# A transformer block pair: the recurrent branch's next projections move into its batches, its block ends into the next preparation, and two attention heads share an output

## What is computed

```python
h = rmsnorm(x, g_mix); z = h @ w_in                      # w_in: 1024 x (672 + 1792 + 2048)
z_mla, z_rwkv, z_gate = split(z)
y_a = mla_branch(z_mla, ...)       # 8 heads: causal softmax(q k^T * scale) @ v, head width 96, v 64
y_b = rwkv7_branch(z_rwkv, ...)    # 8 heads of 64: S_t = S_{t-1} diag(d_t) + (S_{t-1} a_t) b_t^T + v_t k_t^T ; y_t = S_t r_t
gate_a, gate_b = split(sigmoid(z_gate))
x = x + (gate_a * y_a + gate_b * y_b) @ w_out
```

## Time and profile before

| | |
|---|---|
| median of 3 runs | 4001.68 us (3997.36 to 4002.08) |
| the profiled execution | 4002.18 us, span 4000.9 us |
| PE busy | 3722.5 us, 93% of the span |
| DVE, ACT, POOL busy | 45%, 33%, 29% |
| mean granted TensorE clock | 0.957 of full |
| recurrent branch, stages | 49.8 to 1002 us of the span |
| attention | 1107 to 1351 us |

### The profile page before, as it was taken

How to read it: one execution, slowest core, us unless ns; L and a number is a source line. 1 busy time by engine, 2 the same in 40 slices (tenths; PEclk the granted TensorE clock), 3 DMA queues, 4 the chain that set the end, 5 groups by cost and what they waited for, 6 DMA issues and landing times.

```text
span 4000.9 us, 44744 instructions
## 1 busy us (share of the span) xinstructions
PE 3722.5 (93%) x18398; PEld 3068.7 (77%) x18398; DVE 1807.8 (45%) x2380; ACT 1319.3 (33%) x2129; POOL 1167.1 (29%) x624
## 2 busy tenths in 40 slices
PE   5898898979899999999999898999988899999998
PEld 4786887878877777888888666777666778888886
DVE  3435444444155544323332453897543444343435
ACT  3323232232344333122122344776123233232322
POOL 3322313231100232333333112666133322232321
PEclk8988898988999999999999999999999999999999
DMA  4101010000100353111111123222354431111111
GB/s 117 57 1 54 1 47 19 19 29 18 40 12 1 97 162 98 50 48 48 50 50 48 63 90 95 79 74 92 96 159 146 138 95 48 48 48 48 48 48 53
DMA packets 282075, 253.65 MB, mean 63 GB/s; under 512 B 11333, under 2 KB 221569, under 8 KB 281872
## 3 DMA queue, kind: packets, MB, share of 16 engines
q1 hardware_dynamic: 267264, 216.52, 17.9%
q10 hardware_dynamic: 11520, 25.17, 1.6%
q0 software_dynamic: 3088, 9.10, 0.6%
HBM read 214.04 MB, written 36.70 MB: 63 GB/s over the span
## 4 chain that ended last, share of the span: by engine, by line


## 5 line engine op out<-in xcount | busy, mean ns | idle before, releaser
L401 POOL TENSOR_TENSOR weight_lo<-stage,weight_hi 128x1024 fp32r<-128x1024 f32 (+4 forms) x265 | 630.7, 2384 | 1492.9 <-ACT weight_hi L393 1465.3
L364 PE MATMUL psum<-hT_hi,weight_hi 128*128 128x512 f32 x2240 | 893.3, 399 | 13.5 <-ACT sig_g L744 6.6
L365 PE MATMUL psum<-hT_lo,weight_hi 128*128 128x512 f32 x2240 | 879.8, 393 | 0.0
L366 PE MATMUL psum<-hT_hi,weight_lo 128*128 128x512 f32 x2240 | 879.3, 393 | 0.0
L364 PEld LDWEIGHTS psum<-hT_hi,weight_hi 128*128 128x128 f32 x2240 | 426.3, 190 | 111.4 <-issue 14.1
L365 PEld LDWEIGHTS psum<-hT_lo,weight_hi 128*128 128x128 f32 x2240 | 426.1, 190 | 93.2 <-issue 5.8
L366 PEld LDWEIGHTS psum<-hT_hi,weight_lo 128*128 128x128 f32 x2240 | 425.2, 190 | 89.7
L393 ACT ACTIVATE weight_hi<-stage 128x1024 fp32r<-128x1024 f32 (+4 forms) x329 | 315.6, 974 | 466.0 <-PE psum L366 406.6
L1937 DVE TENSOR_TENSOR x<-x,psum 128x512 f32<-128x512 f32 x432 | 289.9, 686 | 215.3 <-PE psum L366 214.7
L364 PE MATMUL psum<-weight_hi,act_hi 128*128 128x512 f32 x864 | 339.2, 393 | 0.0
L366 PE MATMUL psum<-weight_hi,act_lo 128*128 128x512 f32 x864 | 338.9, 392 | 0.0
(11 more groups left out here) (371 smaller groups left out, 5955.3 us busy)
## 6 DMA issues: line engine op xcount, KB each, us to landing
stage<-in_w_in SPq DMA_DIRECT2D x64, 512.0 KB, 4.0
stage<-in_w_up SPq DMA_DIRECT2D x44, 512.0 KB, 3.9
scratch_gates<-gate ACTq DMA_DIRECT2D x64, 256.0 KB, 2.0
gs<-scratch_gates SPq DMA_DIRECT2D x64, 256.0 KB, 2.8
stage<-in_w_out SPq DMA_DIRECT2D x32, 512.0 KB, 4.6
stage<-in_w_ffn_up SPq DMA_DIRECT2D x32, 512.0 KB, 4.1
stage<-in_w_ffn_down SPq DMA_DIRECT2D x32, 512.0 KB, 3.8
stage<-in_w_down SPq DMA_DIRECT2D x22, 512.0 KB, 3.3
```

Of the source, the lines that this page charges most:

```text
L364: q.matmul(out, stat[0], mov[0], start=first, stop=False)
L365: q.matmul(out, stat[0], mov[1], start=False, stop=False)
L366: return q.matmul(out, stat[1], mov[0], start=False, stop=final)
L401: g.q.tensor_tensor(lo, K.staged(w), hi.bitcast(F32), ALU.subtract).then_inc(*S.w_lo_pool.up(w))
```

## The change

- **Recurrent branch.** The z stage of block b+1 leaves its place. Its steps are put behind steps of the batches of block b (`order_batches`): r's first half behind the second `gram` of the first two batches, r's second half and its weight step behind `first`, r's mix behind level 2's product, k's first half behind `carry`; in the other two batches k's second half and weight step behind the second `gram`, k's mix behind level 1, v's halves behind level 3's product and behind `carry`, v's mix at the end. In block 3's batches four gate halves take these places. The end of block b (`finish_0` to `finish_4`) is put between the steps of the preparation of block b+1 (`order_prep`); the waits for the yT store go into a `finish_4` of their own behind the transposes. Gate halves: 6, 8, 6, 6 in the preparations, 4 in the last batches, 2 with the last end. The handover in front of each preparation but the first is that of the batches' end; the one before block 0's z projections and the one behind them go away.
- **Ring.** The weight ring has three slots until the branch ends, five after it; what a slot held is noted in `slot_had`. The intro splits three tiles in place of five. Tiles are now listed as they are taken, in the same order otherwise. `zraw`, `k`, `v` and `tmp` lie where the last two slots will be.
- **Attention.** The units go by query block and head: (7, 0) of head 0, (7, 0) of head 1, (6, 1) of head 0 ... P is scaled by 1/sum on DVE before it is transposed (`scale_p`, a step ahead of the `turn_p` of the unit before). The output of both heads is made together, v (128 x 64) stationary and PT (128 columns) moving, one head into partitions 0 to 63 and the other into 64 to 127 of bank 7. ACT and DVE split it from there into oT; `otok` and `pair_out` go away. PT has four buffers.

```diff
-    if w >= RING:
-        a.wait_ge(S.mm, ("tile", w - RING))
+    if K.slot_had[w] is not None:
+        a.wait_ge(S.mm, ("tile", K.slot_had[w]))
...
+def act_finish_4(K, blk):
+    K.a.wait_ge(K.S.y_store, blk)
+def dve_finish_4(K, blk):
     K.v.wait_ge(K.S.y_store, blk)
...
-QB_ORDER = (7, 0, 6, 1, 5, 2, 4, 3)
+QB_ORDER = ((7, 0), (6, 1), (5, 2), (4, 3))
 TURN_LAG, OUT_LAG = 2, 1
-UNITS = [(pair, h, qb) for pair in range(HEADS // 2) for h in range(2) for qb in QB_ORDER]
+UNITS = [(pair, h, qb) for pair in range(HEADS // 2) for two in QB_ORDER for h in range(2) for qb in two]
...
+def dve_scale_p(K, u):
+    v, S, (pair, h, qb) = K.v, K.S, UNITS[u]
+    rows = K.Pm[u % len(K.Pm)][:, 0:(qb + 1) * P]
+    v.wait_ge(S.act_evac, ("exp", u))
+    v.step(v.q.reciprocal(K.st[:, 3, u:u + 1], K.st[:, 2, u:u + 1]))
+    v.q.tensor_scalar(rows, rows, K.st[:, 3, u:u + 1], None, ALU.mult).then_inc(*S.dve_op.up(("P", u)))
...
-        a.wait_ge(S.mm, ("o", u - len(K.PT)))
+        a.wait_ge(S.mm, ("o", second_head(u - len(K.PT))))
...
+def second_head(u):
+    return u if UNITS[u][1] else u + 2
...
     for j in range(qb + 1):
-        mm = pe.q.matmul(b[:, 0:VDIM], K.PT[u % len(K.PT)][:, j, :], K.vh[pair % 2][:, j, h, :], start=j == 0, stop=j == qb)
+        for h in range(2):
+            mm = pe.q.matmul(b[hd(h), 0:P], K.vh[pair % 2][:, j, h, :], K.PT[(u - 2 + 2 * h) % len(K.PT)][:, j, :],
+                             start=j == 0, stop=j == qb)
     mm.then_inc(*S.mm.up(("o", u)))
...
+def act_output(K, u):
+    a, S, (pair, _, qb) = K.a, K.S, UNITS[u]
+    a.wait_ge(S.mm, ("o", u))
+    a.q.activation(K.oT[0][:, pair, qb * P:(qb + 1) * P], K.bank(("o", u))[:, 0:P], ACT.Copy).then_inc(*S.br_hi.up(("oT", u)))
...
+    hi, lo = (o[:, pair, qb * P:(qb + 1) * P] for o in K.oT)
+    v.wait_ge(S.br_hi, ("oT", u))
+    v.q.tensor_tensor(lo, K.bank(("o", u))[:, 0:P], hi.bitcast(F32), ALU.subtract).then_inc(*S.br_lo_dve.up(("oT", u)))
+    K.free(("o", u), S.br_lo_dve)
...
-    ring = [pair("weight", [P, TILE]) for _ in range(RING)]
+    ring = [pair("weight", [P, TILE]) for _ in range(RWKV_RING)]
+    ring_end = m.lo
+    ring += [pair("weight", [P, TILE]) for _ in range(RING - RWKV_RING)]
...
-RWKV_GATES = (4, 3, 4, 5)
-GATES_LAST = 4
+RWKV_RING = 3
+PREP_GATES = (6, 8, 6, 6)
+LAST_BATCH_GATES = 4
...
+    def take(self, *tiles):
+        self.tiles += tiles
+        return len(self.tiles) - len(tiles)
+    def slot(self, s):
+        self.low.append(self.engines[0])
+        self.engines.append(self.engines.pop(0))
+        self.slot_of.append(s)
+        self.slot_had.append(self.last_in.get(s))
+        self.last_in[s] = self.split
+        self.do("weight", self.split)
+        self.split += 1
     def released(self, n=1):
         for _ in range(n):
-            if self.split < self.tiles:
-                self.low.append(self.engines[0])
...
-    o.released(RING)
+    for s in range(RWKV_RING):
+        o.slot(s)
...
+def order_prep(o, blk, gates):
+    ends = blk > 0
+    gates.open()
+    gates.limit = gates.done + PREP_GATES[blk]
+    o.do("r_copy", blk)
+    o.do("prep_zero", blk)
+    if ends:
+        o.do("finish_0", blk - 1)
+    for h in range(NHALF):
+        o.do("prep_lora", blk, h)
+    o.do("prep_decay", blk)
+    gates.fill(2)
+    if ends:
+        o.do("finish_1", blk - 1)
+    o.do("prep_scan", blk)
+    o.do("prep_scale", blk)
+    o.do("prep_square", blk)
+    gates.fill(1)
+    for h in range(NHALF):
+        o.do("prep_length", blk, h)
+        gates.fill(1)
+    if ends:
+        o.do("finish_2", blk - 1)
+    o.do("prep_key", blk)
+    o.do("prep_bonus", blk)
+    gates.fill(1)
+    o.do("prep_r", blk)
+    o.do("prep_a", blk)
+    o.do("prep_b", blk)
+    o.do("prep_k", blk)
+    if ends:
+        o.do("finish_3", blk - 1)
+    gates.fill(gates.limit - gates.done)
+    for n in range(4):
+        for c0 in range(0, NCH, 4):
+            o.do("tok", blk, n, c0)
+    if ends:
+        o.do("finish_4", blk - 1)
+    gates.close()
+    o.handover()
...
+def order_batches(o, blk, gates):
+    if blk + 1 < NR:
+        r, k, v = (order_z(o, n * NR + blk + 1) for n in range(3))
+        def mix(n):
+            o.do("z_mix", n * NR + blk + 1)
+        behind = {(0, 1): [(advance, r, 1)], (0, 2): [(finish, r)], (0, 5): [(mix, 0)], (0, 17): [(advance, k, 1)],
+                  (2, 1): [(finish, k)], (2, 4): [(mix, 1)], (2, 7): [(advance, v, 1)], (2, 17): [(finish, v)]}
+    else:
+        gates.open(2)
+        gates.limit = gates.done + LAST_BATCH_GATES
+        behind = {(n, at): [(gates.fill, 1)] for n in (0, 2) for at in (1, 2, 17)}
+    o.do("state_zero", blk)
+    for n in (0, 2):
+        running, at = [order_batch(o, blk, n, 0), order_batch(o, blk, n + 1, 1)], 0
+        while running:
+            running = [g for g in running if next(g, "end") != "end"]
+            for do, *what in behind.get((n, at), ()):
+                do(*what)
+            at += 1
+    if blk + 1 < NR:
+        mix(2)
+    else:
+        gates.close()
+    o.handover()
...
 def order_rwkv(o):
     gates = Gating(o, "gates1")
     o.do("rwkv_consts")
-    order_z(o, 12)
+    order_zs(o, 12)
     o.do("lora")
-    order_z(o, 13)
+    order_zs(o, 13)
     o.do("sig_g")
-    o.handover()
     o.do("rwkv_ready")
+    order_zs(o, 0, NR, 2 * NR)
     for blk in range(NR):
-        rest = order_finish(o, blk - 1) if blk else iter(())
-        next(rest, None)
-        order_z(o, blk, rest)
-        o.do("r_copy", blk)
-        order_z(o, NR + blk, rest)
-        order_z(o, 2 * NR + blk, rest)
-        finish(rest)
-        o.handover()
-        gates.open()
-        gates.limit = 2 * sum(RWKV_GATES[:blk + 1]) - (GATES_LAST if blk == NR - 1 else 0)
-        o.do("prep_zero", blk)
-        for h in range(NHALF):
-            o.do("prep_lora", blk, h)
-        o.do("prep_decay", blk)
-        gates.fill(3)
-        o.do("prep_scan", blk)
-        o.do("prep_scale", blk)
-        o.do("prep_square", blk)
-        for h in range(NHALF):
-            o.do("prep_length", blk, h)
-            gates.fill(1 + h)
-        o.do("prep_key", blk)
-        o.do("prep_bonus", blk)
+        order_prep(o, blk, gates)
+        order_batches(o, blk, gates)
+    gates.open()
+    gates.limit = 4 * ND
+    for n in range(4):
+        o.do(f"finish_{n}", NR - 1)
         gates.fill(1)
-        o.do("prep_r", blk)
-        o.do("prep_a", blk)
-        o.do("prep_b", blk)
-        o.do("prep_k", blk)
-        gates.fill(gates.limit - gates.done)
-        for n in range(4):
-            for c0 in range(0, NCH, 4):
-                o.do("tok", blk, n, c0)
-        gates.close()
-        o.handover()
-        o.do("state_zero", blk)
-        for n0 in (0, 2):
-            running = [order_batch(o, blk, n0, 0), order_batch(o, blk, n0 + 1, 1)]
-            while running:
-                running = [g for g in running if next(g, "end") != "end"]
-        o.handover()
-    gates.open()
-    gates.limit += GATES_LAST
-    for _ in order_finish(o, NR - 1):
-        gates.fill(1)
-    gates.fill(GATES_LAST)
+    gates.fill(4 * ND)
+    o.do("finish_4", NR - 1)
     gates.close()
     o.handover()
+    for s in range(RWKV_RING, RING):
+        o.slot(s)
...
+        if 0 <= i - 1 < len(UNITS):
+            o.do("scale_p", i - 1)
...
-        if u >= 0:
+        if u >= 0 and UNITS[u][1]:
             o.do("output", u)
-            if u % (2 * NT) == 2 * NT - 1:
-                for t0 in range(0, NT, 4):
-                    o.do("pair_out", UNITS[u][0], t0)
```

More of the change, by code:

```diff
@@ L628, in act_gate @@
     a, S, key = K.a, K.S, ("gate", name, c, h)
-    store = S.gate_store[name][slot]
+    store = S.gate_store[name][slot % 2]
     a.wait_ge(S.mm, key)
@@ L2593, in one @@
             if h == 0:
-                self.w = self.o.take()
+                self.w = self.o.take(self.tile(c))
             w = self.w
-        self.o.do("gate", self.name, c, w, h, self.slot)
+        self.o.do("gate", self.name, c, w, h, self.base + self.slot)
         self.slot = 1 - self.slot
@@ L2606, with __init__ @@
 class Order:
-    def __init__(self, tiles):
-        self.steps, self.tiles, self.taken, self.split, self.low, self.engines = [], tiles, 0, 0, [], ["G"]
+    def __init__(self, io):
+        self.io, self.steps, self.tiles, self.split, self.back, self.low, self.engines = io, [], [], 0, 0, [], ["G"]
+        self.slot_of, self.slot_had, self.last_in = [], [], {}
         self.handovers, self.relu_order = 0, {}
@@ L2693, in order_z, with order_zs @@
             o.released()
-        if between is not None:
-            next(between, None)
-    o.do("z_mix", c)
-def order_finish(o, blk):
-    o.do("finish_0", blk)
-    yield
-    o.do("finish_1", blk)
-    yield
-    o.do("finish_2", blk)
-    yield
-    o.do("finish_3", blk)
+        yield
+def order_zs(o, *blocks):
+    for c in blocks:
+        finish(order_z(o, c))
+        o.do("z_mix", c)
 def order_batch(o, blk, n, side):
```

(16 more changed lines are left out.)

176 lines of the change are left out of this document (56 added, 120 removed).

## The result

The changed kernel takes 4072.29 us (median of 4 runs, 4067.22 to 4075.82) where the kernel before takes 4001.01: a ratio of 1.018, with a 95% interval of 1.0165 to 1.0189. It is slower, as forecast, but by 71 us and not by 25, and outside the range of 3988 to 4056. The profiled execution spans 4074.5 us, 73.6 more than the one before.

What follows compares the result with a forecast made beforehand. The prediction took TensorE, busy 93% of the span, to bound the kernel. 4002.2 us + 53.5 (recurrent branch) - 29 (attention) = 4026.7, and the median 0.5 lower: 4026 us, with 8 in 10 for 3988 to 4056.

Steps and rivals of the forecast that it cites:

- preparation of block 0: First preparation: no block end to place and no handover in front, so -1.5 us.
- preparations 1 to 3 for z stage and preparation: Blocks 1 to 3: z stage plus preparation of 102.3, 100.3, 101.4 us become preparations of 79, 74, 74: -77 us.
- batches: Batch stages: projections cost +38 us in each of three blocks, gate halves +27 in the last: +141 us.
- last batches' end to the first score: End of block 3: two gate halves fewer (-10.9), then waits for DVE (4.5) and the fourth compressed tile (3.4): -3 us.
- attention: Attention: faster outputs -31, pair_out -7, otok waits -4, against exponent waits +7 and form changes +6: -29 us.
- The stalls: Batches: PE waits for masks queued behind weight_lo on POOL, 5.5 us before level 1, 7.4 before the transposes of first.
- Rival B: Preparation: the block end fits into DVE's gaps, so it stays at 60 us and the kernel takes 3981; chance 0.17.
- POOL's two products 5.9: Preparation: after the long reciprocal POOL's two products take 5.9 us, reaching 67.5 us after the batches' end.
- rival C: Attention: 64-column outputs don't run in pairs, 0.108 us each; attention gains -2 or little more, kernel 4052; chance 0.12.
- The form change: Attention: changing the array's form twice for each of 32 outputs costs 0.09 us each, 64 times: +6 us.
- the +7 for scores that wait for the exponent: Attention: too little PE work between large scores, so the next waits for the previous exponent, some 1 us a pair: +7.
- The rival on the clock: Batch stages: dense projections hold 2.4 GHz through half of the slow-clock time, -26 us, kernel 4000; chance 0.13.

Runs made afterwards that it cites:

- late_split: The changed kernel with weight steps that fall due in a pair of batches held until the last level's mask is on POOL's queue: 4011.2 us.
- early_root: The changed kernel with the block end's square root moved ahead of two gate halves in the preparation: 4049.8 us.
- late_gate: The changed kernel with the lone gate half behind the bonus sums moved behind the decay products: 4057.2 us.
- no_scale: The kernel before with the new attention, but without reciprocal and scaling of P (outputs not divided by their row sums): 3978.7 us.
- guard: all3 plus the first gate tile's weight step in a preparation held until scan, scaling and square are issued: 3960.0 us, 0.9894 of the kernel before.
- lag3: The kernel before with the new attention, and the transposes of P one iteration later (TURN_LAG 3 in place of 2): 3984.7 us.
- guard_lag3: guard with the transposes of P one iteration later (TURN_LAG 3): 3957.0 us, 0.9880 of the kernel before.
- all3: The changed kernel with the edits of late_split, early_root and late_gate together: 3972.4 us, 0.9927 of the kernel before.
- pool_scale: The kernel before with the new attention, and P's scaling product on POOL, the reciprocal left on DVE: 4018.9 us.

## Why the prediction was right or wrong

The sign was right, the size was not. The profiled executions give the sum term by term; the first score comes at 1186.50 us after 1107.24. Of the 49 us that the forecast missed, 27 are in the preparations, 19 in attention and 8 at the branch's end and behind the merge; the batches and the intro gave 4 back.

| term | predicted | measured |
|---|---|---|
| intro (first projection at 43.2, not 49.8) | -6 | -6.6 |
| preparation of block 0 | -1.5 | +7.3 |
| preparations 1 to 3 for z stage and preparation | -77 | -59.2 |
| batches | +141 | +137.4 |
| last batches' end to the first score | -3 | +0.5 |
| attention | -29 | -10.0 |
| from the merge on | 0 | +4.3 |
| sum | +24.5 | +73.7 |

- **Batches: right, down to the parts.** 161 us a stage was forecast and came (160.9, 161.2, 160.9; the last 150.3). The stalls were 5.3 and 7.1 us; late_split shows that the weight step ahead of the masks on POOL is their cause. Its gain was 61 us where the prediction's bound, for the stalls alone, was 52. In the four batch stages PE is idle 47 us less, and busy 10 us less, at 0.92 to 0.94 granted for 0.88 to 0.91; that the missing waits raised the clock is likely and not shown.
- **The block end on the path: right.** L477 came at 18.6 us after the batches' end (18 predicted) and the scan at 28.4 (27); early_root shows that the root's place is what held them. The scan is 1.4 us late, and two rows of DVE's short chain explain it: 0.74 and 1.82 us for products of 16 columns that take 0.17 elsewhere, 2.2 too much. In block 1 they end at 357.83 and 359.69 us, where POOL's `weight_lo` and its square end (357.80 and 359.66). Rival B was out with that: the scan would have had to start before 15 us.
- **The preparation's second half: the step that failed.** The prediction went from r*k (50.7; measured 52.2) by bonus sums, reciprocal and "POOL's two products 5.9" to 67.5, and `Bt` ended at 74.5. It took the two products as starting at the reciprocal's end, as they had in the earlier trace rows. But the half behind the bonus sums is now the sixth, the second half of a tile, and so brings a weight step (before, six halves stood ahead of the sums, and what came behind was the first half of the next tile or nothing). PE can start it only behind the sums, it takes 7.3 us with 3.3 of them at 1.2 GHz, and its `weight_lo` comes to POOL 1.4 us after the reciprocal's end, ahead of all three products. I had counted POOL's queue in the batches and not here. In block 2, `Bt` ends 10.6 us behind the reciprocal's end and not 5.9; this is 4.7 of the 7.7 us by which that preparation missed its 74, and 1.7 came from the first half. late_gate gives back 15 of the 26.6 us that preparations missed (the second and third table rows); all three edits bring those with six halves to 68, under the 74 predicted, because the root is early too. Block 0 shows the same order (11.6 us before L905, where the earlier trace rows has 34.3 for all four blocks), and in addition a wait of 5.3 us for r*k, since five gate halves stand ahead of the bonus sums instead of six.
- **Attention: the mechanism right, one cost missed.** The outputs start 0.0545 us apart (median over pairs; 0.108 to 0.112 before), so 576 of them give back 31 to 33 us where the clock is whole, as predicted, and rival C is out. The form change costs 0.203 us from start to start on either side of an output where 0.109 is normal: 0.09 at each of 64 changes, 6 us, as predicted. The Trainium skill (TensorEngine Tiling (Array Packing), "Tiling Modes", key properties) calls such a change a drain; the trace agrees with a drain of 0.09 us and not with one of a whole matmul, 0.27, by which attention would have been 11 us worse. What failed is the sentence that DVE's `scale_p` goes "beside PE". On average it would: 157 us of 234. But it stands behind the next unit's maximum, and small and large scores alternate. PE waited 13.3 us, and no_scale shows that 11.8 us of the stage go when the scaling goes. The waits for rotated queries grew from 6.9 to 9.3; without the scaling they are still 8.6. From the start of one matmul to the start of the next, PE's steps of over 1 us went from 16.1 us (8) to 31.9 (16), and all others fell by 25.7. In that second sum up to 5 us are lost to the clock, which was at 1.2 GHz for 20.5 us of the stage instead of 10.2. The same attention code took 230.1 us in guard and 231.8 in late_split, with 10.2 and 13.7 us at 1.2 GHz, so some 2 to 4 us of the miss are the clock's. One term erred the other way: the +7 for scores that wait for the exponent came as +1 (3.9 us after 2.9). Without this luck the forecast would have missed attention by 6 us more.
- **Moving the wait was no cure.** In the stretches without projections both engines have little room: in the last pair of the changed kernel PE is busy 34.2 and DVE 31.2 of 39.6 us. In lag3 and guard_lag3 two thirds of the wait for `scale_p` came back as a wait for the exponent, and PE's longer busy time at a lower granted clock took the rest. lag3's expectation calls DVE the bound there; its own figures don't show that.
- **The end of the branch and the merge** missed 3.5 and 4.3 us. No run tests them; they stay open. They are no larger than what profiled executions of the same code differ by: the first score came at 1102.4 to 1107.5 us in the five kernels with the old branch, and the part from the merge on took 2645 to 2658 us over all runs.
- **The rival on the clock** (D) did not come at 4000. The mean of a batch stage did rise (0.91 against 0.89 in the earlier trace rows), but the stage is longer: twice the missing share times its length makes 29 us at 1.2 GHz after 27, so nothing was won back. With the stalls taken out, in late_split, it was 0.94 in block 0, which makes some 18 us at 1.2 GHz, and PE's busy time fell by 2.5 us.

The change is therefore slow by three places in POOL's and ACT's queues, since all3, which moves these alone, is faster than the kernel before, and not by its idea: with the steps moved by a few lines, in guard, the first score comes at 1074.9 us, 32 earlier than in the kernel before, and attention takes 230.1 us, 14 less.

## What to carry to other kernels

A projection isn't only its matmuls: it brings an evacuation, a store and the split of the next weights, and these land on queues whose next entry may be what the whole kernel waits for. When a step is moved, write down for each engine what is queued behind its last instruction, in every place it is moved to; the batches were done so here and came out to 3%; the preparation was not, and its gain was missed by a third. And an engine that is busy for two thirds of a stage on average can still be late, in 11 of 64 units here, if large and small units alternate and its small step stands behind the next unit's large one. Last, when stages are compared across kernels, look at PE's idle and busy time apart: of a loss or a gain of a few us, part may be the clock's.

## What the runs showed of the hardware

- **A scan on DVE stands still while POOL is in a product.** Scans of 128 columns take 0.39 to 0.43 us in the kernel before. In early_root two in each of three blocks took 2.04 to 2.66, each until 0.3 us behind the end of the POOL product that had started just ahead of it, and eight took 6.44 us instead of 2.63; with POOL's work moved away in guard they took 2.63, and three preparations became 8 us shorter together. In the kernel before, L732 took 3.30 us beside a POOL product and 1.28 without. It works the other way round too: in late_gate POOL's L883 started 0.04 us behind the start of DVE's L890, which took 1.22 us, and took 3.38 us itself instead of 2.34. The Trainium skill (SBUF — State Buffer, "SBUF: two separate sides") says that DVE and GpSimd share a pair of ports, that an instruction of DVE with two operands in SBUF takes them as a lock for its whole length, and that the later one is blocked and not slowed. The scan reads two such operands, and the trace agrees: the scan doesn't run slower beside the product, it ends when the product has ended. DVE's maxima, which read PSUM, kept their 1.224 us beside POOL in pool_scale.
- **POOL is a poor place for a row scaling.** 128 x 1024 by a column of factors: 2.84 us on POOL, 0.75 on DVE; at 128 columns 0.60 and 0.29.
- **Two 64-column outputs share the array.** With the stationary operand 128 x 64 and alternating halves of the partitions, 32 instructions started within 1.68 us, 0.054 each (1.97 less the last one's own 0.29), and the next of another form came 0.2 later:

```profile
1268.13 1.97 PE L1598 MATMUL psum<-PT,vh 128*64 128x128 f32 x32
1270.03 1.13 PE L1446 MATMUL psum<-wqkv,cT 128*128 128x256 f32 x4
```
